# Half of a round of modulation pieces moves out of the delta rule's front

## The reference, cut to what matters

```python
mod = jnp.einsum('bd,de->be', silu(c), w_ada) + b_ada       # 1024 -> 6 * 1024
sh1, sc1, g1, sh2, sc2, g2 = jnp.split(mod, 6, axis=-1)
h = rms_norm_2(x, norm1_w) * (1.0 + sc1) + sh1
x = x + g1 * token_mixer(h, ...)                            # delta rule heads, then HGRN2 heads
h = rms_norm_2(x, norm2_w) * (1.0 + sc2) + sh2
x = x + g2 * moe(h, ...)
```

```python
L = where(strict, (kb @ kc.T) * decay, 0)                   # inverse of (L + I) is needed
v_new = u - w @ S
o = (qc * exp(gc)) @ S + (qc @ kc.T * decay) @ v_new
S = S * exp(gl) + k_tail.T @ v_new
```

## Time and profile before

| what | us |
|---|---|
| median of three runs | 1682.32 |
| lowest and highest | 1681.39, 1684.59 |
| the profiled execution's own time | 1676.29 |
| its span | 1674.6 |
| PE busy, share | 1503.5 (90%) |
| DVE busy, share | 998.9 (60%) |
| ACT busy, share | 678.1 (40%) |
| median from issue to landing of a piece's load (256 KB) | 4.1 |

### The profile page before, as it was taken

The page is one execution under the profiler, slowest core; times in us unless marked ns, Lnnn a source line. Parts: engine busy times, 40 slices in busy tenths (PEclk is TensorE's granted clock), DMA queues, the critical chain, the costliest instruction groups (busy, mean ns, idle before and its releaser), DMA issues. The chain is left out here.

```text
span 1674.6 us, 29909 instructions
## 1 busy us (share of the span) xinstructions
PE 1503.5 (90%) x12200; PEld 1251.9 (75%) x12200; DVE 998.9 (60%) x1545; ACT 678.1 (40%) x938; POOL 144.8 (9%) x255
## 2 busy tenths in 40 slices
PE   6988688899999989978458889999999999999996
PEld 6976386899999989948338757777777777777774
DVE  5655564576776458655655635666566566666653
ACT  4341332546443344512535324444444444444442
POOL 8000000001000001000111201111111111110000
PEclk9986699899999999979677889999999999999998
DMA  7522400344554648360232758888888988888880
GB/s 248 177 101 76 127 4 3 126 177 162 196 197 163 181 90 163 135 202 1 88 115 104 247 206 332 334 331 336 330 333 336 342 338 340 333 339 335 342 327 25
DMA packets 113225, 349.32 MB, mean 209 GB/s; under 512 B 9634, under 2 KB 33393, under 8 KB 96449
## 3 DMA queue, kind: packets, MB, share of 16 engines
q1 hardware_dynamic: 103184, 315.75, 52.5%
q0 software_dynamic: 8240, 27.40, 5.2%
q10 hardware_dynamic: 1664, 4.26, 0.7%
HBM read 345.15 MB, written 2.23 MB: 207 GB/s over the span
## 5 line engine op out<-in xcount | busy, mean ns | idle before, releaser
L3035 DVE TENSOR_TENSOR weights_lo<-raw_weights,weights_hi 128x2048 fp32r<-128x2048 f32 x99 | 223.8, 2289 | 79.9 <-ACT weights_hi L2935 79.9
L2935 ACT ACTIVATE weights_hi<-raw_weights 128x2048 fp32r<-128x2048 f32 x99 | 185.5, 1910 | 21.1 <-DMA raw_weights<-in_w_gate 17.7
L2736 PE MATMUL bank<-x_hi,weights_hi 128*128 128x256 f32 x544 | 155.1, 285 | 0.0
L2737 PE MATMUL bank<-x_lo,weights_hi 128*128 128x256 f32 x544 | 155.0, 285 | 0.0
L2738 PE MATMUL bank<-x_hi,weights_lo 128*128 128x256 f32 x544 | 154.9, 285 | 0.0
L413 PE MATMUL bank<-in_x_hi,in_w_hi 128*128 128x256 f32 (+2 forms) x456 | 133.5, 293 | 3.6 <-DVE in_w_lo L362 3.6
L413 PE MATMUL bank<-in_x_hi,in_w_lo 128*128 128x256 f32 (+2 forms) x456 | 131.9, 289 | 0.0
L413 PE MATMUL bank<-in_x_lo,in_w_hi 128*128 128x256 f32 (+2 forms) x456 | 131.6, 289 | 0.0
L2816 PE MATMUL bank<-raw_weights,gathered_pair 128*64 128x512 f32 x512 | 113.4, 595 | 0.0
L1536 DVE TENSOR_TENSOR ffn_weights_lo<-weight_ring,ffn_weights_hi 128x2048 fp32r<-128x2048 f32 x33 | 75.6, 2292 | 53.4 <-ACT ffn_weights_hi L1531 53.4
L2736 PEld LDWEIGHTS bank<-x_hi,weights_hi 128*128 128x128 f32 x544 | 105.4, 194 | 2.3 <-issue 1.6
(11 more groups left out here) (618 smaller groups left out, 3738.4 us busy)
## 6 DMA issues: line engine op xcount, KB each, us to landing
raw_weights<-in_w_gate SPq DMA_DIRECT2D x64, 1024.0 KB, 8.8
raw_weights<-in_w_up SPq DMA_DIRECT2D x64, 1024.0 KB, 9.0
raw_weights<-in_w_down SPq DMA_DIRECT2D x64, 1024.0 KB, 8.1
weight_ring<-in_w_in SPq DMA_DIRECT2D x17, 2048.0 KB, 9.1
mixer_memory<-in_w_ada SPq DMA_DIRECT2D x96, 256.0 KB, 4.1
weight_ring<-in_w_ffn_in SPq DMA_DIRECT2D x22, 1024.0 KB, 6.6
weight_ring<-in_w_ffn_out SPq DMA_DIRECT2D x5, 2048.0 KB, 7.8
weight_ring<-in_w_out SPq DMA_DIRECT2D x4, 2048.0 KB, 7.5
```

Of the source, the lines that this page charges most:

```text
L2736: T.matmul(out_, hi[:, d, cut], x_hi[:, d, :], start=(d == 0), stop=False)
L2737: T.matmul(out_, hi[:, d, cut], x_lo[:, d, :], start=False, stop=False)
L2935: S.activation(w_hi[:, n % 4, :], raw_w[:, k % RAW, :], ACT.Copy).then_inc(s_hi.sem, 1)
L3035: V.tensor_tensor(w_lo[:, n % 4, :], raw_w[:, k % RAW, :], w_hi[:, n % 4, :].bitcast(F32), ALU.subtract).then_inc(s_lo.sem, 1)
```

## The change

The front keeps the first 16 pieces of the second round. The other 16 are used in pairs at four places of the chain (before the products of lines 2131, 2146, 2161 and 2173) and the last eight in the first gated norm, after its sums, together with the round's copy, turn and addition. The scalings `kg` and `qg` move from the front to the chain, behind the right hand sides. SP issues 22 loads of the round in the front, 8 in the chain, and in the norm the last 2 and then, once the round has been turned, the first 6 loads of the third round, which the levels' stage no longer issues.

```diff
-                for n in range(ROUND, 2 * ROUND):
+                for n in range(ROUND, ROUND + 22):
                     ada_load(sp, ada_w2, n)
...
-                dve.wait_ge(act_s.sem, act0 + 2)
-                dve_s.on(V.tensor_tensor(kg, mats(k2), eg, ALU.mult))
-                dve_s.on(V.tensor_tensor(qg, mats(q2), eg, ALU.mult))
...
-                for n in range(ROUND + 16, 2 * ROUND):
-                    ada_use(pe, ada_w2, n, bank[7])
-                ada_turn(pe, ada_w2, 1, bank[6])
...
-                ada_add(dve, 1, bank[6])
-
-            @block.scalar
-            def _(act):
-                ada_copy(act, ada_w2, 1, bank[7])
...
+            @block.sync
+            def _(sp):
+                for n in range(ROUND + 22, ROUND + 30):
+                    ada_load(sp, ada_w2, n)
+
+            def pieces(pe, at):
+                for n in range(ROUND + 16 + at, ROUND + 18 + at):
+                    ada_use(pe, ada_w2, n, bank[7])
...
+                marks["rhs"] = dve_s.value
+                dve_s.on(V.tensor_tensor(kg, mats(k2), eg, ALU.mult))
+                marks["kg"] = dve_s.value
+                dve_s.on(V.tensor_tensor(qg, mats(q2), eg, ALU.mult))
...
-                pe.wait_ge(dve_s.sem, dve_s.value)
+                pe.wait_ge(dve_s.sem, marks["rhs"])
...
+                pieces(pe, 0)
                 pe.wait_ge(act_s.sem, act_s.value)
...
+                pieces(pe, 2)
+                pe.wait_ge(dve_s.sem, marks["kg"])
                 pe.wait_ge(act_s.sem, act_s.value)
...
+                pieces(pe, 4)
                 pe.wait_ge(dve_s.sem, dve_s.value)
...
+                pieces(pe, 6)
                 pe.wait_ge(act_s.sem, act_s.value)
...
+        def rest_of_round(sp):
+            for n in range(ROUND + 30, 2 * ROUND):
+                ada_load(sp, ada_w2, n)
+            sp.wait_ge(s_ada_turn.sem, 2)
+            for n in range(2 * ROUND, 2 * ROUND + 6):
+                ada_load(sp, ada_w2, n)
+
+        def end_of_round(pe):
+            for n in range(ROUND + 24, 2 * ROUND):
+                ada_use(pe, ada_w2, n, bank[7])
+            ada_turn(pe, ada_w2, 1, bank[6])
...
+                   beside={"sync": rest_of_round, "tensor": end_of_round, "scalar": lambda act: ada_copy(act, ada_w2, 1, bank[7]),
+                           "vector": lambda dve: ada_add(dve, 1, bank[6])})
...
-                for n in range(2 * ROUND, 3 * ROUND):
+                for n in range(2 * ROUND + 6, 3 * ROUND):
                     ada_load(sp, ada_w2, n)
```

More of the change, by code:

```diff
@@ L2185, in build, with gated_norm @@
         oAh = oA.rearrange("p (h c) t -> p h (c t)", c=2)
-        def gated_norm(o, sq, norm, gate, gain, dst, per_head):
+        def gated_norm(o, sq, norm, gate, gain, dst, per_head, beside={}):
             with nc.Block() as block:
@@ L2223, in _ @@
                     dve_s.on(V.tensor_tensor(dst, dst, sq, ALU.mult))
+                for engine in ("sync", "tensor", "scalar", "vector"):
+                    if engine in beside:
+                        {"sync": block.sync, "tensor": block.tensor, "scalar": block.scalar, "vector": block.vector}[engine](beside[engine])
+        def rest_of_round(sp):
[8 more added lines that the diff above has]
+            ada_turn(pe, ada_w2, 1, bank[6])
         gated_norm(oAh, WW2.rearrange("p a b c -> p (a b c)").rearrange("p (h t) -> p h t", h=GH), gcB, gate_a,
-                   lambda h: param("gdn_norm_w_2"), o_all[:, 0:GH, :], True)
+                   lambda h: param("gdn_norm_w_2"), o_all[:, 0:GH, :], True,
+                   beside={"sync": rest_of_round, "tensor": end_of_round, "scalar": lambda act: ada_copy(act, ada_w2, 1, bank[7]),
+                           "vector": lambda dve: ada_add(dve, 1, bank[6])})
         mh, mh2 = Memory(m2b.tensor, 0, MIX2B), Memory(m2.tensor, 0, MIX2)
```

## The result

The changed kernel took 1669.38 us (median of six runs, 1659.10 to 1673.28), the kernel before beside it 1681.86 (1678.19 to 1686.83): a ratio of 0.991, 95% interval 0.9882 to 0.9938, or 12.5 us off where 12.1 were forecast and 1670.2 given as the time. Repeated later with twelve runs it was 1666.86 against 1681.25, ratio 0.9924 (0.9894 to 0.9955). Two of the later executions (2164.17 us of the kernel before, 1921.58 of six_in_preparation) fell in a slow state with a lower granted clock and are left out of medians and ratios.

What follows compares the result with a forecast made beforehand. The prediction took 32 pieces of 256 KB each to pace front and levels, with the arithmetic waiting. Its terms, -8.3 + 0 + 0.5 + 1.0 - 5.3 = -12.1 us, took 1682.32 to 1670.2 us, range 1663 to 1677.

Steps and rivals of the forecast that it cites:

- Front, -8.3: Front: without the second 16 pieces the inverse starts right behind DVE's last step, 8.3 us earlier, 1 us either way.
- Inverse, 0: Inverse: same instructions and the same 6.3 us at the half clock, so 0, between minus 2.9 and plus 2.9 us.
- Chain, +0.5: Chain: four pairs of pieces added, only pair two bare, scalings free; plus 0.5 us, between 0 and 1.6.
- Norm, +1.0, with -0.6 for full clock sums: First gated norm: SP's late issues end it, plus 1.0 us; minus 0.6 if the sums run at the full clock.
- Levels, -5.3: Levels: six of 32 loads already landed, six pieces' transfer time saved, minus 5.3 us, between minus 2.3 and minus 8.8.
- Sum: Whole kernel: all stage terms together give -12.1 us, so 1670.2 us; this forecast had 51%.
- A: Rival, levels: the head start is spent at once and they gain only 2.3 us; 1673.2 us in total, 22%.
- B: Rival: VectorE becomes the levels' bound, 8.8 us gained there, norm's sums at the full clock; 1665.1 us, 17%.
- C: Rival: front's removed work returns as waits for late pieces in chain and norm, levels gain nothing; 1680 to 1683, 6%.
- D: Rival, inverse: TensorE stays at the half clock to its end, making the kernel slower, 1695.6 us; 4%.

Runs made afterwards that it cites:

- six_in_preparation: The changed kernel with the third round's six early loads issued in the preparation of the HGRN2 heads instead of the norm's end: 1668.93 us, ratio 0.9924.
- no_head_start: The changed kernel without the early loads, all 32 loads of the third round in the levels' stage: 1672.50 us, ratio 0.9951.
- turn_alone: The kernel before with only the eight transposes moved ahead, behind the first six pieces, all 32 pieces still in the front: 1678.68 us, ratio 1.0004.
- scalings_alone: The kernel before with only kg and qg moved from the front to the chain: 1682.06 us, ratio 1.0013.
- turn_after_six: six_in_preparation with the front's eight transposes after the first six pieces instead of all sixteen, ten pieces behind them: 1659.37 us, ratio 0.9891.
- changed_again: The changed kernel itself, run again for its spread beside the variants: 1666.86 us, ratio 0.9924.
- no_later_loads: six_in_preparation without the third round's other 26 loads, so the third part of the modulation is not computed from its weights: 1664.97 us, ratio 0.9912.

## Why the prediction was right, point by point

- *Front, -8.3.* Right, mechanism and size: in the pair of traces 9.3, of which 1.0 is that the first 16 pieces landed sooner. Over six kernels with the changed front 25.2 us against 34.0 over three with the old one: 8.8. no_head_start, which has every part but the early loads, is 8.2 us below the kernel before by the ratio and 8.8 by the medians. The order that I took as given, transposes behind 16 pieces, was itself a wait of 8 us; I read the 6.89 us in front of line 2092 and left it there.
- *Inverse, 0.* 36.2 against 36.6 us, -0.4 (six and three traces), inside the bounds; turn_alone's 35.52, with pieces in front, lies below both, so the 0.4 is no more than the scatter. The Trainium skill advises against idle gaps between bursts of matmuls (TensorE: Matmul & The Clock Gate, section "Why this matters for your kernels"). The traces agree in part: with the gap mostly filled by full products the inverse began at the full clock, where with the gap open it began at 0.50, but the clock then fell all the same and the gain was 0.8 us at most. It says nothing against the change, since the old inverse too began with 6.3 us at the half clock.
- *Chain, +0.5.* +0.7, in all seven kernels that have the bare pair, and 0.66 of it goes when that pair alone is moved. Shown. No piece came late: no wait for a DMA stands in it. The scalings cost nothing: shown by scalings_alone.
- *Norm, +1.0, with -0.6 for full clock sums.* The sums did run at the full clock, and it became +0.7 (-0.1 in the second trace). With the sums at the full clock the prediction's working gives 1.0 - 1.8 = -0.8, and the traces gave more. The step that failed is the time of SP's chain behind the sums: that chain runs through the landings of pieces 30 and 31 (used 3.2 and 4.4 us after the first of their loads was issued, where I took 3.0), the copy and the turn, which took 1.11 us at the half clock that it met. That SP ends the stage was right. Without the six issues the norm takes 11.76 us with the sums at the full clock: the issues cost 1.2 and 2.0 us in the two traces.
- *Levels, -5.3.* The direction and the start of the stage were right, the term too large: -3.1 in the pair, -3.2 over eight and four traces, -5.8 in the best. That all six loads' transfer time would come off the stage assumed that DMA paces it to its end. Only the gain at its start came in every trace: the first products of line 2424 start 4.36 us into the stage in all eight with early loads, and 6.0 to 6.6 in the four without. The last products came 2.6 us earlier on average, with waits of TensorE for VectorE (1.57 in front of L2447) where it had waited for pieces. What the term left out is the granted clock, which the stage's length follows: with early loads 37.10 us at 0.77, 35.78 at 0.87 and 33.04 at 0.95; without them 40.95 at 0.69 and 38.85 at 0.76. How much of the 3.2 us is the head start itself, and how much a higher clock, is not separated beyond the 2 us at the start.
- *Sum.* The terms as measured over all traces, -8.8 - 0.4 + 0.7 + 0.3 - 3.2 = -11.4, lie 1 to 3 us short of the medians' -12.5 and -14.4. The norm's +0.3 is the mean of its two traces. Where the rest is stays open, and code that no edit touches varies by more than that: in the thirteen traces the front is reached after 712 to 721 us, the second norm takes 12.2 to 13.5, and all that follows the levels 814 to 819. The levels fell 2.1 us short of the forecast; the front (0.5), the inverse (0.4) and the norm (0.7) came out better by 1.6 together and nearly cancelled it, with 0.2 against from the chain. So the 0.8 us between forecast and result is partly luck, and less than two medians of the same kernel differ by. The extremes of the prediction's sum (1678.5 and 1661.7) leave out the 1 us either way that it gives the front; with it they are 1679.5 and 1660.7.
- *Rivals.* A was nearest in the levels, where the mean gain was 3.2 against its 2.3. B's bound, the stage without DMA, is 30 us and isn't reached. C and D did not happen.

turn_after_six goes further than the change in the same direction; its total is 20.2 us below the kernel before by the medians and 18.3 by the ratio. Its interval overlaps that of the changed kernel, while its front is 7 us shorter and nothing else longer than in the other variants.

## What to carry to other kernels

Filler work belongs in a stage only up to the length of what the stage must do anyway; and within it, an engine's own critical step goes ahead of filler that waits for DMA, as soon as its operands are ready. When a stage ends with all engines meeting, count the issuing engine's list too: six DMA issues behind a late wait cost 1.2 to 2.0 us here, and none where they stood in a stage with nothing else for that engine. In these traces a head start of transfers was worth the wait at the stage's start each time, and further gain only in part. Before the length of a stage is put down to an edit, compare the granted clock of the two traces in it.

## What the runs showed of the hardware

SP's issues of 256 KB loads took 2.7 us for six in the norm (turn done at 802.48, last issue done at 805.21) and 3.48 for six at the front's start. A stage of the same 724 matmul records took 33.04 us at a mean clock of 0.95 and 35.78 at 0.87 in two executions of the same kernel. The same sums ran in 1.99 us at 2.4 GHz and in 3.68 to 3.78 at 1.2 GHz, and which of the two they met changed between kernels whose code is the same up to them: full in changed, changed_again and no_head_start, half in six_in_preparation and no_later_loads. Without SP's six issues the norm took 11.76 us with them at the full clock and up to 13.24 at the half one, a difference as large as most edits of this study.
